# A two-layer hybrid decoder step: sample score passes, key loads and evacuations put in another order in the mixing stage

## What is computed

```python
def layer_fwd(x, pos0, pool_prefix, ret_s0, past_k, past_v, ...):
    x = x + 0.5 * swiglu(rmsnorm(x, g_ffn1), f1_in, f1_out)
    z = rmsnorm(x, g_mix) @ w_in
    u, qa, ka, va, qr, kr, vr, gr = jnp.split(z, offs, axis=-1)
    y_pool, pool_new = pool_mixer(u, pool_prefix, pos, pool_w, pool_scale)   # windows 2, 4, 8, 16
    kf, vf = (past_k, ka), (past_v, va)                                      # joined along time
    y_att = moba_seq(qa, kf, vf, pos)             # 6 heads, blocks of 256 keys, the best 3 + own
    o_r, ret_new = retention(qr, kr * HEAD_DIM ** -0.5, vr, ret_s0)          # 6 heads, decay per head
    o_r = o_r * lax.rsqrt(jnp.mean(o_r * o_r, axis=-1) + EPS)
    y_ret = jax.nn.silu(gr) * o_r
    x = x + jnp.concatenate([y_pool, y_att, y_ret], axis=-1) @ w_out
    x = x + 0.5 * swiglu(rmsnorm(x, g_ffn2), f2_in, f2_out)
    return x, ka, va, pool_new, ret_new
```

## Time and profile before

| | us |
|---|---|
| median of three runs | 1438.18 (1436.74 to 1443.50) |
| the profiled execution | 1442.09 |
| its span, first to last instruction | 1440.1 |
| mixing stage of layer 0 / layer 1 | 271.8 to 475.8 / 971.8 to 1176.2 |

### The profile page before, as it was taken

The page is one execution under the profiler, slowest core; times in us unless marked ns, Lnnn a source line. Parts: engine busy times, 40 slices in busy tenths (PEclk is TensorE's granted clock), DMA queues, the critical chain, the costliest instruction groups (busy, mean ns, idle before and its releaser), DMA issues.

```text
span 1440.1 us, 28345 instructions
## 1 busy us (share of the span) xinstructions
PE 1353.8 (94%) x11129; PEld 1296.4 (90%) x11129; DVE 811.3 (56%) x870; ACT 650.3 (45%) x715; POOL 216.7 (15%) x343
## 2 busy tenths in 40 slices
PE   6999999899877999999999999989987789999998
PEld 4999999898646899999999999989974589999997
DVE  4655545478573655554455555456866546555444
ACT  4655533334223555553455554432433245555343
POOL 3000001370334100000100000034313611000001
PEclk9999999999978999999999999999998799999999
DMA  6444445754858344444444444474646744444443
GB/s 206 152 146 146 142 154 186 200 166 128 256 144 277 117 147 151 154 151 138 157 147 154 147 146 135 161 238 139 209 130 202 255 156 145 146 146 146 137 159 121
DMA packets 210896, 235.27 MB, mean 163 GB/s; under 512 B 14975, under 2 KB 203145, under 8 KB 210805
## 3 DMA queue, kind: packets, MB, share of 16 engines
q1 hardware_dynamic: 200828, 204.90, 44.1%
q0 software_dynamic: 9856, 29.14, 6.5%
q10 hardware_dynamic: 120, 0.03, 0.0%
HBM read 228.83 MB, written 5.32 MB: 163 GB/s over the span
## 4 chain that ended last, share of the span: by engine, by line
PE 88%; DVE 7%; issue 2%; DVEq 2%; ACT 1%; DMA 0%; SPq 0%; ACTq 0%
PE ps L1233 22%; PE ps L1234 22%; PE ps L1235 22%; PE ps L1315 4%; PE ps L1317 3%; PE ps L1316 3%; PE ps L1456 2%; DVE kbuf L990 2%; PE ps L1494 2%; DVEq L1163 1%; PE ps L1629 1%; PE ps L1444 1%; PE ps L1630 1%; PE ps L1631 1%; DVE w_lo L844 0%
## 5 line engine op out<-in xcount | busy, mean ns | idle before, releaser
L587 ACT ACTIVATE w_hi<-w_raw 128x2048 fp32r<-128x2048 f32 x170 | 325.6, 1915 | 538.2 <-PE ps L1235 425.5
L844 DVE TENSOR_TENSOR w_lo<-w_raw,w_hi 128x2048 fp32r<-128x2048 f32 x170 | 391.4, 2302 | 208.6 <-ACT w_hi L587 205.9
L1233 PE MATMUL ps<-h_hi,w_hi 128*128 128x320 f32 x768 | 241.3, 314 | 9.3 <-DVE w_lo L844 3.5
L1234 PE MATMUL ps<-h_lo,w_hi 128*128 128x320 f32 x768 | 239.8, 312 | 0.0
L1235 PE MATMUL ps<-h_hi,w_lo 128*128 128x320 f32 x768 | 239.7, 312 | 0.0
L1233 PE MATMUL ps<-g_hi,w_hi 128*128 128x320 f32 x704 | 218.4, 310 | 1.2 <-DVE g_lo L851 1.2
L1234 PE MATMUL ps<-g_lo,w_hi 128*128 128x320 f32 x704 | 217.7, 309 | 0.0
L1235 PE MATMUL ps<-g_hi,w_lo 128*128 128x320 f32 x704 | 217.7, 309 | 0.0
L1234 PE MATMUL ps<-act_lo,w_hi 128*128 128x320 f32 x704 | 217.5, 309 | 0.0
L1233 PE MATMUL ps<-act_hi,w_hi 128*128 128x320 f32 x704 | 217.5, 309 | 0.0
L1235 PE MATMUL ps<-act_hi,w_lo 128*128 128x320 f32 x704 | 217.5, 309 | 0.0
(11 more groups left out here) (271 smaller groups left out, 1900.0 us busy)
## 6 DMA issues: line engine op xcount, KB each, us to landing
w_raw<-in_ffn_w_in SPq DMA_DIRECT2D x90, 1024.0 KB, 5.1
w_raw<-in_ffn_w_out SPq DMA_DIRECT2D x32, 896.0 KB, 4.6
kbuf<-in_cache_k SPq DMA_DIRECT2D x128, 192.0 KB, 3.4
w_raw<-in_w_in SPq DMA_DIRECT2D x22, 1024.0 KB, 5.5
w_raw<-in_ffn_w_out SPq DMA_DIRECT2D x16, 1024.0 KB, 5.0
kbuf<-in_cache_v POOLq DMA_DIRECT2D x64, 192.0 KB, 3.8
w_raw<-in_w_out SPq DMA_DIRECT2D x8, 1024.0 KB, 7.8
v_c<-in_cache_v POOLq DMA_DIRECT2D x32, 192.0 KB, 3.3
```

The source lines that it names most:

```text
L587: act.activation(w_hi[:, slot, :], w_raw[:, slot, :], ACT.Copy).then_inc(hi_done, 1)
L844: dve.tensor_tensor(w_lo[:, slot, :], w_raw[:, slot, :], w_hi[:, slot, :].bitcast(F32), ALU.subtract).then_inc(split_done, 1)
L1233: pe.matmul(out, w_hi[:, slot, w], hi[:, k, :], start=(k == 0), stop=False)
L1234: pe.matmul(out, w_hi[:, slot, w], lo[:, k, :], start=False, stop=False)
```

## The change

On PE, the four sample passes move: pass 0 from behind chunk 5 to behind chunk 4 (with `scores(0)` now behind chunk 5), pass 1 from behind chunk 9 to behind chunk 8, pass 2 to behind `att_out(2)` and one value transposition, pass 3 from behind `transpose_probs(0)` to in front of `smp_state(2)`. `scores(1)` and `scores(2)`, `transpose_p` and a few token transpositions go along; the banks of two transpositions change so that this is possible. The early out-projection with chunk 12 moves from in front of pass 2 with V to behind `transpose_out(2)`. DVE's and ACT's lists are put in the order that belongs to it. A fourth buffer, `sp_d`, lies in slot 0 of `w_lo`. SP loads the first half of the first keys in front of FFN1's output weights, the keys of pass 1 in front of mix weight 8, and weights 9 and 10 in front of the store of the values.

```diff
-        sp = [sp_a, sp_b, sp_c, sp_a]
+        sp_d = at("sp_d", [96, PAST_LEN + SMP], F32, w_lo_at, 0)
+        sp = [sp_a, sp_b, sp_c, sp_d]
# SP
                 ffn_in(A["ffn1_w_in"], L, C_F1I, 1)
+                sp_e.wait_ge(loaded, 16 * len(C))
+                load_k(0, 0, 0)
                 ffn_out(A["ffn1_w_out"], L, C_F1O)
...
-                sp_e.wait_ge(loaded, 16 * len(C))
-                for half in range(2):
-                    load_k(0, 0, half)
+                load_k(0, 0, 1)
...
                 for c in range(3, 8):
                     mix_load(c)
+                next_k(1, 0)
+                next_k(1, 1)
+                mix_load(8)
                 sp_e.wait_ge(u_out, 2 * L + 2)
...
-                mix_load(8)
-                next_k(1, 0)
                 sp_e.wait_ge(ka_out, 3 * L + 2)
                 store_kv(0, "k", ka_tok, None, stored_k)
-                next_k(1, 1)
                 mix_load(9)
+                mix_load(10)
                 sp_e.wait_ge(va_out, 3 * L + 2)
                 store_kv(0, "v", va_tok, None, stored_va)
-                mix_load(10)
                 mix_load(11)
# GpSimd: qprep(0) behind the first pooling window (n == 0) and not the second;
# qprep(3) behind load_v_all(1) and not behind spread_v(3)
# ScalarE
-                exps(0)
                 mix_hi(10)
                 att_evac(0)
+                exps(1)
+                mix_hi(11)
+                ka_tokens(2)
                 probs_out(2)
                 probs_out(3)
                 exp(4)
                 exp(5)
-                mix_hi(11)
-                ka_tokens(2)
+                att_evac(1)
                 va_tokens(2)
...
                 act.wait_ge(stored_u, 32 * (L + 1))
+                exps(2)
                 for f in range(3):
                     ret_square(f)
...
-                exps(2)
                 probs_evac(0)
-                for f in range(3):
-                    or_high(f)
+                exps(3)
                 out_evac(0, 0)
                 out_evac(0, 1)
                 probs_evac(1)
+                for f in range(3):
+                    or_high(f)
                 y_high(0)
-                exps(3)
-                mix_hi(12)
# VectorE, from chunk 8 on (the order after)
                 evac_last(8)
+                mix_lo(10)
                 normalise(2)
                 normalise(3)
                 soft_sum(0)
+                dve.wait_ge(pool_d, L + 1)
+                soft_in(1)
+                evac_first(9)
+                soft_bias(1)
+                evac_last(9)
+                mix_lo(11)
                 smax(4)
                 dve.drain()
                 smax(5)
+                evac_first(10)
+                turn_k(2, 0, 0)
+                evac_last(10)
+                turn_k(2, 0, 1)
                 dve.wait_ge(past_done, L + 1)
                 for half in range(2):
                     ins = dve.tensor_copy(o_past[half][:], ...)
                 ins.then_inc(past_ok, 1)
-                mix_lo(11)
                 normalise(4)
                 normalise(5)
...
                 decay_mask(1)
+                soft_sum(1)
+                dve.wait_ge(chunk_used, L * C_ALL + (C_MIX + 14))
+                soft_in(2)
+                soft_bias(2)
+                turn_k(3, 0, 0)
                 for t in range(2):
                     dve.wait_ge(pool_hi, 2 * L + (t + 1))
...
-                mix_lo(12)
+                y_rest(1)
+                dve.wait_ge(pt2_done, NB * L + 8)
+                mix_lo(12)
# TensorE
                 mix(8)
                 pe.wait_ge(va_out, 3 * L + 2)
                 att_out(0)
+                pe.wait_ge(s_max, H * L + 4)
+                sample_scores(1)
                 mix(9)
                 wait_apart(pe, oa_out, 3 * L + 1)
                 tokens(ZKA, 2, 7).then_inc(ka_tr, 1)
+                transpose_p(2)
+                transpose_p(3)
+                scores(2)
+                past_states()
                 mix(10)
                 pe.wait_ge(ka_out, 3 * L + 3)
                 att_out(1)
+                wait_apart(pe, past_ok, L + 1)
+                tokens(ZVA, 2, 3).then_inc(va_tr, 1)
+                mix(11)
...
                 ret_out(2)
+                sample_scores(3)
                 smp_state(2)
-                wait_apart(pe, sm_in, L * 4 + 3)
+                wait_apart(pe, sm_in, L * 4 + 4)
                 mean_squares()
                 wait_apart(pe, r_mask, H * L + 6)
                 transpose_probs(0)
-                wait_apart(pe, o_std, 3 * L + 3)
-                sample_scores(3)
```

More of the change, by code:

```diff
@@ L340, in _, with load_k @@
                 ffn_in(A["ffn1_w_in"], L, C_F1I, 1)
+                def load_k(p, bb, half):
+                    page = page_numbers(mybir.EngineType.SP, p * 16 + (8 * bb + 4 * half), 4)
+                    for j in range(4):
+                        sp_e.dma_start(kbuf[bb][:, 4 * half + j, :],
+                                       A["cache_k"][L, page[j]].rearrange("t h d -> t (h d)")).then_inc(k_landed[bb][half], 16)
+                sp_e.wait_ge(loaded, 16 * len(C))
+                load_k(0, 0, 0)
                 ffn_out(A["ffn1_w_out"], L, C_F1O)
@@ L352, in store_kv @@
                                        own).then_inc(landed, 16)
[L354 to L358, removed]
                 def next_k(p, bb):
@@ L553, in _ @@
                 load_v_all(1)
+                wait_apart(pool, own_done, L * 4 + 3)
+                qprep(L, 3)
+                pool.drain()
                 wait_apart(pool, oa_done, 3 * L + 3)
@@ L738, in _ @@
                 ka_tokens(1)
+                exps(0)
                 exp(0)
@@ L1055, in _ @@
                 evac_first(3)
-                turn_k(0, 0, 1)
+                turn_k(0, 1, 1)
                 evac_last(3)
                 mix_lo(5)
-                dve.drain()
-                dve.tensor_copy(q_smp[:], z[:, ZQA:ZQA + 3, SEQ:]).then_inc(q_own, 1)
                 evac_first(4)
-                turn_k(0, 1, 0)
                 evac_last(4)
+                mix_lo(6)
+                soft_in(0)
+                evac_first(5)
+                soft_bias(0)
+                evac_last(5)
+                mix_lo(7)
                 smax(0)
@@ L1066, in _ @@
                 smax(1)
-                mix_lo(6)
-                evac_first(5)
-                turn_k(0, 1, 1)
-                evac_last(5)
-                mix_lo(7)
+                evac_first(6)
+                turn_k(1, 0, 0)
+                evac_last(6)
+                mix_lo(8)
                 normalise(0)
                 normalise(1)
-                soft_in(0)
-                evac_first(6)
-                soft_bias(0)
-                evac_last(6)
+                turn_k(1, 0, 1)
+                evac_first(7)
+                turn_k(1, 1, 0)
+                evac_last(7)
+                mix_lo(9)
+                turn_k(1, 1, 1)
                 smax(2)
@@ L1113, in _ @@
                 ins.then_inc(past_ok, 1)
-                mix_lo(11)
                 normalise(4)
                 normalise(5)
-                dve.wait_ge(pool_d, L + 1)
-                dve.wait_ge(stored_k, 32 * L + 16)
-                soft_in(1)
-                evac_first(10)
-                soft_bias(1)
-                evac_last(10)
                 evac_last(11)
+                turn_k(2, 1, 0)
+                turn_k(2, 1, 1)
                 dve.wait_ge(stored_k, 32 * (L + 1))
@@ L1147, in _ @@
                 decay_mask(3)
+                turn_k(3, 0, 1)
                 gate(0)
-                soft_in(2)
+                decay_mask(4)
+                turn_k(3, 1, 0)
                 new_state(0)
-                decay_mask(4)
+                decay_mask(5)
+                turn_k(3, 1, 1)
                 gate(1)
                 new_state(1)
-                decay_mask(5)
                 gate(2)
+                soft_in(3)
                 new_state(2)
-                soft_sum(1)
-                soft_bias(2)
+                soft_sum(2)
+                soft_bias(3)
                 def or_norm(f):
@@ L1176, in y_rest @@
                     ins.then_inc(ys_low, 1)
-                for half in range(2):
-                    turn_k(3, 0, half)
-                or_norm(0)
-                for half in range(2):
-                    turn_k(3, 1, half)
-                soft_in(3)
-                soft_sum(2)
-                soft_bias(3)
-                or_norm(1)
-                or_norm(2)
+                for f in range(3):
+                    or_norm(f)
                 y_rest(0)
```

100 lines of the change are left out of this document (37 added, 63 removed).

## The result

| | before | after |
|---|---|---|
| median of four runs, us | 1437.46 (1436.09 to 1443.50) | 1455.14 (1451.24 to 1457.33) |
| profiled execution / its span | 1442.09 / 1440.1 | 1454.61 / 1452.6 |
| after : before | | 1.0112, 95% interval 1.0075 to 1.0148 |

The kernel became about 18 us slower by the medians and 16 by the ratio, where I had forecast 1434 us (1422 to 1446). It is outside the range, on the side of rival B, whose own number was 1447.

What follows compares the result with a forecast made beforehand. TensorE was taken as busy nearly always outside each layer's mixing stage, where waits and the lower clock cost time. A gain of 2.2 us a layer, 4.4 in all, off the median of 1438.18 gave 1434 us, range 1422 to 1446.

Steps and rivals of the forecast that it cites:

- rival B: VectorE's queue becomes the bound, clock down from chunk 11 to pass 3; 8.8 us lost in all, 1447 us; chance 0.18.
- Units: Step times read from the profile: 7.1 us a mix chunk, 4.6 a sample pass, 10.1 for a set of VectorE work.
- pass 0: First sample pass, now at chunk 4: starts at 303.4 and waits for nothing; pure reordering, 0 us.
- pass 1: Second sample pass, now at chunk 8: starts at 342.7 after waiting 1.4 us; 3.7 us gained by chunk 10.
- keys around FFN1: Four first-key page loads ahead of FFN1's output weights: taken as 0, at most 2 x 2.6 us lost.
- weights: Weight 8 loaded behind the keys of pass 1: hidden with 4 us of cover, 0 us.
- Mixing's end: Before chunk 11 TensorE waits 6.0 us for o_past; ret_scores(0) starts at 376.8, so 2.9 us lost against before.
- pool_low: New wait of 5.8 us in front of ret_out(0), behind VectorE's longer queue.
- Retention: From ret_out(0) to the first V product: ends at 424.0, half way between 418.8 and 429; before 424.36.
- The last passes with V: End of the stage: o_tok's 7.3 us wait goes, GpSimd's V units start 1.9 earlier; 2.2 us gained a layer.
- A: Rival: full clock kept in retention, 7.4 us gained a layer, 14.8 in all, 1423 us; chance 0.22.
- C: Rival: V loads hold the end wherever retention ends; 0 to 3 us gained in all, 1437 us; chance 0.15.

Runs made afterwards that it cites:

- e15: The changed kernel with mix weight 8 loaded in front of the keys of pass 1, as before the change; 1454.00 us, ratio 1.0088 to the kernel before.
- e5: The changed kernel with everything from VectorE's decay_mask(1) on as before the change, and GpSimd's qprep(3) again after spread_v(3); 1439.43 us, ratio 0.9989.
- e10: The kernel before with only SyncE's queue as changed, up to next_k(2, 0); 1452.72 us, ratio 1.0072.
- e13: The changed kernel with the o_past copy right behind evac_last(9) and chunk 10's first tile evacuated before the softmax maxima; 1444.02 us, ratio 1.0019.
- e9: The changed kernel with GpSimd's qprep(3) moved behind spread_v(1), nothing else; 1455.17 us, ratio 1.0101.
- e6: The changed kernel with VectorE's pool_low, decay masks and gate(0) ahead of soft_in(2), and ScalarE's ret_square(0) ahead of exps(2); 1454.26 us, ratio 1.0075.
- e1: The changed kernel with everything from VectorE's decay_mask(1) on as before the change, GpSimd's qprep(3) still ahead of V unit 0's loads; 1462.85 us, ratio 1.0158.
- e2: The changed kernel with the early out-projection back between V passes 1 and 2 and sp_d moved off chunk 12's low part; 1448.05 us, ratio 1.0060.
- e14: The changed kernel with 38 extra products, their result unused, in TensorE's wait for pool_low; 1447.17 us, ratio 1.0045.

## Why the prediction was wrong, by its steps

- **Units, pass 0, pass 1, keys around FFN1, weights**: right. Pass 0 began at 303.48 (303.4), pass 1 at 342.53 (342.7, waiting 0.6 of 1.4). Weight 8 behind the keys cost nothing here (e15), and the front with all of SyncE's new order nothing either (e5); e10 shows on what that rests: the 4 us of cover that I counted for weight 8 come from pass 0's new place, which I hadn't said.
- **Mixing's end**: right. The wait for o_past was 4.3, not 6.0, and `ret_scores(0)` started at 377.25, forecast 376.8: 3.4 us lost there against before, forecast 2.9. Taking the wait away gives more than its length, 5.5 us a layer (e13).
- **pool_low**: wait 5.8, forecast 5.8. What I did not see is GpSimd's queue. `qprep(3)` was moved in front of the loads of V unit 0 and the spread, and the forecast prices that nowhere. Behind the pool_low wait it cost nothing (e9); without that wait it became the next bound at once (e6, e1).
- **Retention**: failed. "I take 424.0, half way" between 418.8 at the full clock and 429 at the lower one. The clock was not half way: it was 0.50 without a break from 396.8 to 413, up to the key products of pass 3. TensorE took until 426.7, so this is 2.7 us a layer of the miss; rival B's point of 429.9 wasn't reached. The far bound of 429 was also summed too low: 395.7 and the 34.8 us named with it are 430.5.
- **The last passes with V**: failed, and the larger part; this is where the forecast had its gain of 2.2 us a layer. The wait for o_tok went, as forecast. Forecast 42.3 us from the first V product to the late out-projection (424.0 to 466.3), measured 47.4: 5.1 a layer. The waits that the moved out-projection no longer covers were named and too small (hand-over 2.5 instead of 1.7, unit 5 3.2 instead of 1.4, chunk 12's low part 2.6 instead of 2.1), and the clock behind them was priced at nothing: three V units took 3.1 to 3.6 us instead of 1.95, and about the first third of the early out-projection with chunk 12 took 0.47 instead of 0.31 a product. With the out-projection put back (e2) the same stretch takes 42.9. I had credited GpSimd's earlier start, but the first V product came 2.7 us later than forecast and ran at the lower clock, and `transpose_probs(1)` with it, so that unit 4 was issued at 434.96, not 430.2; before it was 432.08.
- **Sum**: 2 x (2.7 + 5.1) = 15.6 us of the 16.9 between the forecast span (1440.1 less 4.4) and the measured one. The rest lies between the two mixing stages (496.5 us, before 496.0) and behind the second (264.7, before 263.9); its cause stays open.
- **Rivals**: A's clock did not come, C's "0 to 3 us out of GpSimd" neither. A's 7.4 us a layer do not come out of its own terms (432.08 less 417.9, 5.4 and 0.8 is 8.0), which moves its 1423 by 1. B had the right side and the right engine, but its 1447 is 8 us short and its mechanism only half right: the clock did not stay down from chunk 11 on, pass 2 ran at 1.00 (380 to 391), and it let only retention and FFN2's first chunk pay for the clock.
- **Signs**: of those named, a granted clock in retention below 0.65 (0.60) and a mixing stage more than 4 us from 202 (209.7) came, and both spoke against the forecast; so did a last V unit that was issued later, not earlier.

## What to carry to other kernels

Price a wait on TensorE together with the work behind it at the lower clock: here waits of 4.3 and 6.0 us a layer cost 5.5 and 11.7 us a layer of the kernel's time (e13, and e1 against e5). When a waiting step is moved up in any engine's list, write down what stands behind it, on GpSimd too; a wait that is hidden by another one shows only when that one is mended, so that single experiments say "no gain" twice and the pair says otherwise. And don't move filler work out from between two hand-overs for the sake of one that goes.

## What was unexpected of the hardware

Products whose result nobody reads made the kernel 8 us faster (e14). In retention of the changed kernel TensorE was busy 16.15 of 16.2 us at the lower level and stayed there (396.8 to 413.0), while in e5 the same products ran at the upper one up to 405: what the clock does depends on what stood in front of them.
